# The last two units ahead of three norms in halves of the tokens, and low parts in the raw weights' place

## What is computed

```
def _rms_norm(x, g):
    return x * lax.rsqrt(jnp.mean(x * x, axis=-1, keepdims=True) + NORM_EPS) * g

def _layer(x, st, P, l):
    xn = _rms_norm(x, P['norm_mix_pre'][l])
    cols = xn @ P['w_in'][l]
    ...
    mix = merged @ P['w_out'][l]
    x = x + _rms_norm(mix, P['norm_mix_post'][l])
    xn = _rms_norm(x, P['norm_ffn_pre'][l])
    gate, up = _split(xn @ P['w_ffn_in'][l], [D_FF, D_FF])
    f = (silu(gate) * up) @ P['w_ffn_out'][l]
    x = x + _rms_norm(f, P['norm_ffn_post'][l])
```

## Time and profile before

| | us |
|---|---|
| median of 3 runs | 2446.35 (2445.53 to 2447.68) |
| the profiled execution | 2449.73 |
| its span, first to last instruction | 2447.9 |
| TensorE busy | 2335.9 |
| VectorE, ScalarE, GpSimd busy | 994.4, 863.1, 786.7 |
| granted TensorE clock, mean | 0.977 |

### The profile page before, as it was taken

One profiled execution on the slowest core, in us unless ns is written; L12 is line 12 of the kernel. 1 busy time (PEld: TensorE's weight loads), 2 busy tenths in 40 slices (PEclk: granted clock), 3 DMA queues, 4 the chain that ended last, 5 costly groups with the idle time before them and its releaser, 6 DMA issues.

```text
span 2447.9 us, 53310 instructions
## 1 busy us (share of the span) xinstructions
PE 2335.9 (95%) x23450; PEld 2224.4 (91%) x23450; DVE 994.4 (41%) x1559; ACT 863.1 (35%) x1442; POOL 786.7 (32%) x630
## 2 busy tenths in 40 slices
PE   7999989999999899999989999999999989999997
PEld 7998878988899899999989988888888989999997
DVE  4435654454434522220073376455443624332102
ACT  4345532213344522222244455222313544222222
POOL 3432322112235244444424332221212433444441
PEclk9999989999999999999989999999999999999998
DMA  5432211111124132233325221112113242332331
GB/s 164 128 88 74 57 40 32 28 49 32 42 69 145 58 90 87 87 91 87 83 93 136 61 74 53 32 28 49 32 28 83 68 129 61 90 92 87 88 88 52
DMA packets 334190, 180.80 MB, mean 74 GB/s; under 512 B 33528, under 2 KB 330648, under 8 KB 332936
## 3 DMA queue, kind: packets, MB, share of 16 engines
q1 hardware_dynamic: 333776, 177.34, 26.1%
q10 hardware_dynamic: 184, 0.05, 0.0%
HBM read 167.98 MB, written 9.38 MB: 72 GB/s over the span
## 4 chain that ended last, share of the span: by engine, by line
PE 82%; DVE 11%; ACT 4%; issue 2%; DMA 1%; POOL 0%; DVEq 0%; ACTq 0%; SPq 0%; POOLq 0%
PE psum_products L658 72%; PE psum_mixer L658 8%; DVE xn_low L2050 1%; DMA w_raw<-in_w_in 1%; DVE merged L2044 1%; DVE squares L1641 1%; DVE gate_product L2042 1%; DVE xn_low L1638 0%; ACT c_in_rate L1222 0%; ACT w_high L1222 0%; ACT c_kprime L1222 0%; DVE c_kappa_r L1753 0%; DVE c_in_rate L1754 0%; ACT L1222 0%; PE psum_mixer L1037 0%
## 5 line engine op out<-in xcount | busy, mean ns | idle before, releaser
L2273 POOL TENSOR_TENSOR w_low<-w_raw,w_high 128x512 fp32r<-128x512 f32 (+2 forms) x606 | 761.8, 1279 | 1557.7 <-ACT w_high L1222 1557.1
L658 PE MATMUL psum_products<-xn_high,w_high 128*128 128x272 f32 (+1 forms) x3424 | 738.6, 297 | 28.8 <-DVE xn_low L1623 12.3
L658 PE MATMUL psum_products<-xn_high,w_low 128*128 128x272 f32 (+1 forms) x3424 | 710.7, 289 | 0.0
L658 PE MATMUL psum_products<-xn_low,w_high 128*128 128x272 f32 (+1 forms) x3424 | 708.9, 289 | 0.0
L658 PEld LDWEIGHTS psum_products<-xn_high,w_high 128*128 128x128 f32 x3424 | 542.9, 189 | 50.6 <-issue 26.2
L658 PEld LDWEIGHTS psum_products<-xn_low,w_high 128*128 128x128 f32 x3424 | 543.0, 190 | 0.0
L658 PEld LDWEIGHTS psum_products<-xn_high,w_low 128*128 128x128 f32 x3424 | 539.7, 190 | 0.0
L1222 ACT ACTIVATE w_high<-w_raw 128x1024 fp32r<-128x1024 f32 (+2 forms) x303 | 303.2, 1003 | 174.6 <-PE psum_products L658 144.3
L658 PE MATMUL psum_products<-hidden_high,w_high 128*128 128x272 f32 x704 | 145.9, 288 | 0.0
L658 PE MATMUL psum_products<-hidden_high,w_low 128*128 128x272 f32 x704 | 145.7, 288 | 0.0
L658 PE MATMUL psum_products<-hidden_low,w_high 128*128 128x272 f32 x704 | 145.1, 288 | 0.0
(11 more groups left out here) (374 smaller groups left out, 3008.9 us busy)
## 6 DMA issues: line engine op xcount, KB each, us to landing
w_raw<-in_w_in SPq DMA_DIRECT2D x112, 512.0 KB, 4.0
w_raw<-in_w_ffn_in SPq DMA_DIRECT2D x88, 512.0 KB, 3.8
w_raw<-in_w_ffn_out SPq DMA_DIRECT2D x32, 512.0 KB, 3.9
w_raw<-in_w_out SPq DMA_DIRECT2D x16, 512.0 KB, 4.0
w_raw<-in_w_ffn_out SPq DMA_DIRECT2D x16, 384.0 KB, 3.4
x_kept<-x SPq DMA_DIRECT2D x2, 2176.0 KB, 7.5
x<-x_kept SPq DMA_DIRECT2D x2, 2176.0 KB, 9.7
w_raw<-in_w_in SPq DMA_DIRECT2D x16, 256.0 KB, 3.9
```

The costliest lines, as they stand in the source:

```text
L658: return pe.matmul(out, lhsT, rhs, start=start, stop=stop, skip_group_check=True)
L2273: low_ready.inc(pool.tensor_tensor(wl[:, n % NSPLIT, ks_], wraw[:, slot, ks_], wh[:, n % NSPLIT, ks_].bitcast(F32), ALU.subtract))
```

## The change

1. The last two units ahead of a `norm_post` (`mix` 6 and 7; of `ffn_out` block 7 its parts 1 and 2) run in halves of the tokens (`two_halves`): all of the first unit and of the second for tokens 0 to 271, then the same for tokens 272 to 543, with each half's ones-sums between. Three norms are halved; the last one, ahead of the output, is not.
2. `norm_post` on VectorE and the `norm_pre` behind it take blocks 0 to 5 for the first half, blocks 0 to 5 for the second half, then blocks 6 and 7 whole (`STEPS`, 14 steps in place of 8). Ln and Exp are taken for each half by itself; ScalarE evacuates the second half of the last unit, and takes its Ln and Exp, between the third and the fifth step.
3. `w_low` has the memory of `w_raw`: GpSimd writes the low part over the raw weights. NRAW = 5, NSPLIT = 4, splits up to unit u + 4, and a raw slot is free when its product is done. `split_both` is gone; the splits that fell there are issued by ScalarE inside `norm_pre` at block 6 ("midst").
4. `cols_a` 16 loads 32 and 96 columns where it loaded 4 and 4.

```diff
-NRAW, NSPLIT = 3, 3
+NRAW, NSPLIT = 5, 4
...
+BY_HALF = 6
+BOTH = (0, 1)
+STEPS = [(k, (0,)) for k in range(BY_HALF)] + [(k, (1,)) for k in range(BY_HALF)] + [(k, BOTH) for k in range(BY_HALF, KD)]
+def halved(l, w_):
+    return w_ in (1, 3) and (l, w_) != (DEPTH - 1, 3)
+def steps_from(l, w_):
+    return [(k, BOTH) for k in range(KD)] if (l, w_) == (0, 0) else STEPS
+def by_halves(s):
+    return (s[0] == "mix" and s[2] >= KD - 2 and halved(s[1], 1)
+            or s[0] == "ffn_out" and s[2] == KD - 1 and s[3] >= 1 and halved(s[1], 3))
...
-    wraw = fixed("w_raw", [P, NRAW, 8, P])
+    wraw_at = region(4 * NRAW * 8 * P)
+    wraw = place("w_raw", [P, NRAW, 8, P], wraw_at)
-    wl = fixed("w_low", [P, NSPLIT, 8, P], F32R)
+    wl = place("w_low", [P, NRAW, 8, P], wraw_at, F32R)
...
-        ahead, made = {}, 3
+        ahead, made = {}, 4
-                upto = sum(unit_no[t] <= u + (3 if s in split_no else 2) for t in split_units)
+                upto = sum(unit_no[t] <= u + 4 for t in split_units)
-                if plan[i + 1][0] == "norm_post":
-                    at_ = plan[i + 1]
+                if by_halves(s):
+                    at_ = ("midst", s[1] + (s[0] == "ffn_out"), 2 if s[0] == "mix" else 0)
-                ahead[at_] = list(range(made, max(made, upto)))
+                ahead.setdefault(at_, []).extend(range(made, max(made, upto)))
-        by_vec = [n for i, s in enumerate(plan) if s[0] == "norm_post" for n in ahead[s]]
...
-                return [cols(a["w_in"], 4 * A_W, A_H, 0), cols(a["w_in"], 4 * A_W + A_H, A_H, 32)]
+                return [cols(a["w_in"], 4 * A_W, 32, 0), cols(a["w_in"], 4 * A_W + A_H, 96, 32)]
...
-            def gemm(s, rh=None, rl=None, rhs=None, first=True, last=True, cut=HALF, wait_k=False, k0=0, nk=8, steps=8):
-                ks = range(done_k.get(s, 0), min(nk, done_k.get(s, 0) + steps))
+            def gemm(s, rh=None, rl=None, rhs=None, first=True, last=True, cut=HALF, wait_k=False, k0=0, nk=8, steps=8,
+                     bs=BOTH, late=False):
+                there = done_k.get((s, bs[0]), 0)
+                ks = range(there, min(nk, there + steps))
-                done_k[s] = ks[-1] + 1
+                for b in bs:
+                    done_k[s, b] = ks[-1] + 1
...
-                                  (wl[:, slot, k], rh[:, k0 + k])]
+                                  (wl[:, unit_no[s] % NRAW, k], rh[:, k0 + k])]
+                            if b not in bs:
+                                continue
-                    products.inc(last_mm)
+                    if 1 in bs:
+                        products.inc(last_mm)
+                    elif last:
+                        flow("first_half").inc(last_mm)
-            def product(s, steps=8):
+            def product(s, steps=8, bs=BOTH, late=False):
...
-                bank[0].claim(pe)
-                bank[1].claim(pe)
-                for k in range(KD):
+                for i, (k, bs) in enumerate(steps_from(l, w_)):
-                        product(s, 1)
-                    pe.wait_ge(sq_ready.sem, norm_base(l, w_) + k + 1)
-                    for b in range(2):
+                        product(s, 1, bs, late=(l, w_) != (0, 0))
+                    if i == 1 and (l, w_) != (0, 0):
+                        last_sum(*((l, 1) if w_ == 2 else (l - 1, 3)), 1)
+                    pe.wait_ge(sq_ready.sem, norm_base(l, w_) + i + 1)
+                    for b in bs:
+                        if k == 0:
+                            bank[b].claim(pe)
...
-            def post_sums(l, w_):
+            def post_sums(l, w_, bs=BOTH, wait=True):
-                flow("squares_added").wait_next(pe, "pe")
-                bank[0].claim(pe)
-                bank[1].claim(pe)
-                for b in range(2):
+                if wait:
+                    flow("squares_added").wait_next(pe, "pe")
+                for b in bs:
+                    bank[b].claim(pe)
+                for b in bs:
+            def last_sum(l, w_, b):
+                src = squares if w_ == 1 else sq2
+                if b == 0:
+                    flow(f"first_squares_{w_}").wait_next(pe, "pe", 2 if w_ == 1 else 1)
+                else:
+                    flow("last_squares").wait_next(pe, "pe")
+                bank[b].filled(mm(mp[b][:, 0:HALF], C("ones"), src[:, KD - 1, b * HALF:(b + 1) * HALF], start=False), "act")
+            def two_halves(l, w_, one, two, nk):
+                one(8, (0,))
+                two(nk - 2, (0,))
+                post_sums(l, w_, (0,))
+                two(2, (0,))
+                one(3, (1,))
+                last_sum(l, w_, 0)
+                one(8, (1,))
+                two(nk - 2, (1,))
+                post_sums(l, w_, (1,), wait=w_ == 1)
+                two(2, (1,))
+                if halved(l, w_):
+                    return
...
+            def factor_log(w_, b):
+                dst = rstd_of(w_)
+                bank[b].read(act, "act")
+                step(fn(dst[:, tokens((b,))], mp[b][:, 0:HALF], ACT.Ln, scale=1.0 / D, bias=C("scalars", 0, 1)), bank[b].empty["act"])
+            def factor_exp(w_, b):
+                dst = rstd_of(w_)
+                step(fn(dst[:, tokens((b,))], dst[:, tokens((b,))], ACT.Exp, scale=-0.5), flow("rstd"))
+            def out_half(s, b):
+                sq, y = (squares, mixed) if s[0] == "mix" else (sq2, ffn_y)
+                if b == 0:
+                    flow("first_half").wait_next(act, "act")
+                    pair = tiles[s[:3] if s[0] == "ffn_out" else s][0]
+                else:
+                    pair = product_done(s)
+                src = gp[:, 2 * pair + b, 0:HALF]
+                name = "last_squares" if b else "first_squares_1" if s[0] == "mix" else "first_squares_3"
+                (sq_ready if b and s[2] < KD - 1 else flow(name)).inc(fn(sq[:, s[2], tokens((b,))], src, ACT.Square))
+                step(fn(y[:, s[2], tokens((b,))], src, ACT.Copy), emptied["act"] if b else None)
+            def norm_post(l, w_):
+                if not halved(l, w_):
+                    factor(rstd_of(w_))
+                    return
+                factor_log(w_, 0)
+                factor_exp(w_, 0)
+                if w_ == 1:
+                    out_half(("mix", l, KD - 2), 1)
-                for k in range(KD):
+                post = (l, 1) if w_ == 2 else (l - 1, 3)
+                for i, (k, bs) in enumerate(steps_from(l, w_)):
+                    n = tokens(bs)
-                    xh_ready.inc(fn(hi[:, k, :], x[:, k, :], ACT.Copy, scale=prm[:, l, g0 + k:g0 + k + 1]))
-                    sq_ready.inc(fn(squares[:, k, :], x[:, k, :], ACT.Square))
-                    if l == 0 and w_ == 0 and k < 3:
+                        if i == 2:
+                            out_half(("mix", l, KD - 1) if w_ == 2 else ("ffn_out", l - 1, KD - 1, 2), 1)
+                    xh_ready.inc(fn(hi[:, k, n], x[:, k, n], ACT.Copy, scale=prm[:, l, g0 + k:g0 + k + 1]))
+                    sq_ready.inc(fn(squares[:, k, n], x[:, k, n], ACT.Square))
+                    if l or w_:
+                        if i == 2:
+                            factor_log(post[1], 1)
+                        if i == 3:
+                            factor_exp(post[1], 1)
+                        if k == BY_HALF and bs == BOTH:
+                            for u in ahead.get(("midst", l, w_), ()):
+                                split_high(u)
+                    elif k < 4:
...
-            def split_both(n):
-                s = split_units[n]
-                dve.wait_ge(products.sem, unit_no[split_units[n - NSPLIT]] + 1)
-                at, value = landed_at[s]
-                dve.wait_ge(landed[at].sem, value)
-                nk, slot = nk_of(s), n % NSPLIT
-                raw = wraw[:, unit_no[s] % NRAW, 0:nk]
-                step(dve.tensor_copy(wh[:, slot, 0:nk], raw))
-                step(tt(wl[:, slot, 0:nk], raw, wh[:, slot, 0:nk].bitcast(F32), SUB), vec_ready)
-                for n in ahead[("norm_post", l, w_)]:
-                    split_both(n)
+                order = STEPS if halved(l, w_) else [(k, BOTH) for k in range(KD)]
+                second = order.index((0, (1,))) if halved(l, w_) else None
-                def scaled(k):
-                    step(stt(out=tmp[:, k, :], in0=src[:, k, :], scalar=prm[:, l, g0 + k:g0 + k + 1], in1=rstd[:],
+                def scaled(i):
+                    k, bs = order[i]
+                    n = tokens(bs)
+                    if i == second:
+                        flow("rstd").wait_next(dve, "dve")
+                    step(stt(out=tmp[:, k, n], in0=src[:, k, n], scalar=prm[:, l, g0 + k:g0 + k + 1], in1=rstd_of(w_)[:, n],
-                for k in range(KD):
-                    step(tt(x[:, k, :], x[:, k, :], tmp[:, k, :], ADD), flow("x_new"))
-                    if k + 1 < KD:
-                        scaled(k + 1)
+                for i, (k, bs) in enumerate(order):
```

(57 more changed lines are left out.)

57 lines of the change are left out of this document (31 added, 26 removed).

## The result

The changed kernel takes 2454.3 us (median of 11 executions, 2452.2 to 2462.7), the kernel before 2447.7 (11, 2445.1 to 2453.3). The ratio is 1.003, with a 95% interval of 1.0018 to 1.0042: some 7 us slower. The forecast was 2453.3. The profiled execution has a span of 2452.5 us.

A forecast was written before the change was run, and what follows sets the result against it. TensorE, busy 95% of the span, bounds the kernel. Norm stages +3.4, clock +4.5, weight ring -2.0 and +1.0 make +6.9 us on the profiled 2449.73, which lies 3.4 above the median: 2453.3, own range 2449 to 2459, wider range 2437 to 2464.

The forecast's parts named there:

- The wait at the turn: TensorE's idle time between the last product and the norm's first step goes, 6.8 us a norm, and the clock stays up.
- The half step of 1.64 us: In the norm stage VectorE sets the pace, not TensorE: twelve half steps of 1.64 us, 19.7 in place of 14.6.
- ScalarE's detours: Half steps three to five: evacuating the second half, two table loads, Ln and Exp delay the roundings by 2.8 us.
- The tail: Full step 6 of the norm stage: two weight splits and the Ln table ahead of the last rounding, 2.4 us late.
- GpSimd, 0.4: GpSimd's low parts beside the norm's last steps slow VectorE by 0.4 us, bounds 0 and 0.9.
- The sums: Norm stages at full clock: mix norm 44.2 against 43.1 us, ffn norm 43.0 against 41.8; three norms +3.4.
- The clock behind the tail: TensorE idles about 2.5 us ahead of its last step; slow clock then costs 1.5 us a norm (0 to 3.0).
- The ring: The new weight slots: -2.0 for an earlier load, +1.0 for late landings, 0 for waits in the third mixers.
- (a): First layer: the weight load ScalarE stood 11.1 us for is issued a whole queue earlier, -2.0 us.
- (b): Third branch's stage: mix weights' splits find loads about 1 us short, big low parts run beside VectorE's; 0.5 a layer, +1.0.
- (c): Third mixers, 340 to 645: TensorE's waits for low parts, 4.5 us a layer, give back 0 of 9.0.
- The faster one: Norm stages: ScalarE's delays and late splits don't hold VectorE up and the clock stays; -12 in all, 2434; chance 0.20.

The follow-up runs named there:

- factor2_dve: Changed kernel with the second half's factor left out: two linear VectorE instructions replace ScalarE's inverse root, so part of the computation is missing; 2454.3 us.
- splits_last: Changed kernel with the two weight splits of a norm's full step 6 issued behind the stage's last rounding and squares; 2449.15 us.
- ring_only: Kernel before with only the new weight ring (five raw slots holding the low part, four high slots) and wider columns of cols_a 16; 2447.75 us.
- half4_last: Changed kernel with four blocks in halves, not six, and the norm's two weight splits behind the stage's last squares; 2448.9 us.
- by_half_4: Changed kernel with four blocks in halves and four whole behind each norm, in place of six and two; 2455.5 us.
- half4_last_root: half4_last with all norm factors made by square root on ScalarE and reciprocal on VectorE in place of Ln and Exp; 2442.9 us.
- ring_moved: ring_only with two weight splits a layer issued later, behind the second mixer's last chunk and the third mixer's first steps; 2448.3 us.

## Why the prediction came out, point by point
- **The wait at the turn goes.** Right in place, and the clock at the turn stays up; it is at 0.50 from 811 to 813.5, behind waits of up to 1.2 us, where VectorE sets the pace. But TensorE's idle time is the same, in nine waits.
- **The half step of 1.64 us, VectorE as the pace.** Exact: 1.64 in the chain, the half add 0.44, scale and low part 0.50. By the Trainium skill's 60 ns (Perfetto Trace Analysis, "Optimizing Scalar/DVE Operations") I had estimated 0.39 for the add, and the trace doesn't agree. I had passed over what the same passage adds, that a profiled instruction shows about twice this overhead: with 120 ns the estimate is 0.42, near the measured 0.44.
- **ScalarE's detours, 2.8 us late.** From the third add to the fifth rounding's end it is 802.62 to 809.64, 7.0 us against 6.7: 3.2 late. factor2_dve, which takes out the two tables and Ln and Exp, wins 1.2 to 1.3 us a stage at like clock, not the 1.9 that I then expected of it.
- **The tail, 2.4 late.** The last two roundings end 4.75 us apart (4.8 forecast), TensorE's gap is 2.3 (2.5). splits_last shows that the splits make 2.1 of it.
- **GpSimd, 0.4.** 0.3 in place, so the term was right for this order of issue, and its upper bound of 0.9 for one instruction was right as well. What I didn't see is that the tail kept the other instructions out of it: with the splits earlier it is 3.7 us of VectorE's time and 2.65 of the stage's. The Trainium skill (SBUF — State Buffer, "SBUF: two separate sides") has the two engines take turns on a port pair for whole instructions; 1.7 in place of 0.75 us, and back at 0.79 when GpSimd's work is cut to an eighth, agree with it.
- **The sums.** Without the clock's part the stages grew by 1.8, 1.8 and 2.0, where I had 1.1, 1.2 and 1.1: the term that was too small, by 2.2 in all. In the first norm two of its parts make up the miss: the first scale comes 11.0 us behind mix 6's first matmul (787.40 to 798.42) where I had 10.4, and the detours are 0.4 over.
- **The clock behind the tail, 1.5 each.** 1.6 behind the first norm, 1.5 behind the second (12 matmuls and the sums against 1.78 and 0.92), nothing behind the third, with the same gap: 3.1 of 4.5.
- **The ring, -2.0, +1.0 and 0.** (a) was -3.0. (b) was named wrongly: not landings in the merge stage, but whole splits ahead of a_out_high and c_tanh_w, 2.4 to 2.9 us a layer. Of (c) 2.1 us a layer came back, not nothing. I had put a change of over 3 us in the mixers' length as a sign against me: from the third mixer's first step to its last group's it is 4.2 in the changed kernel, but only 1.0 in ring_only, which has the same work there, so most of the 4.2 belongs to that execution. The parts summed to -1.0; ring_only gives 0.0, with an interval of -2.2 to +2.4, so the sum stands and its parts don't.
- **The total.** The forecast was 1.0 us low, and that it is so near is luck, since three errors cancel: the stages came to +8.8 for +7.9, the rest of the profiled execution to -4.2 for -1.0, and the profiled execution is itself the median now, where I had taken 3.4 off. The norms' costs and their places, the larger part of the forecast, are what was right.
- **The rivals.** The faster one, whose time should read 2433 for 2434 by its own sum, needed tail and detours without effect: they are there in the chain. With the tail gone (splits_last, half4_last) the kernel is where it was before, not faster.

## What to carry to other kernels
Halving a stage to cover one wait pays only while the slower engine's instructions shrink with it: here the fixed 155 ns of each VectorE instruction, the second set of table loads and the moved splits together cost 6.5 us more than the covered wait gave. With those splits moved behind the stage and four blocks in halves the stages were 4.0 us shorter than before (half4_last), and the time was the same. Work that is put off to make room lands on another chain; look what it stands ahead of, and which engine it shares a port with, before choosing its place. Where a kernel waits little, a gain of a few us must be read with the granted clock beside it: what looked like by_half_4's win in the stages was the clock's alone.

## What the runs showed of the hardware
- VectorE instructions with two inputs in SBUF took 1.67 to 1.76 us in place of 0.72 to 0.79 beside GpSimd, on 272 elements 1.26 to 1.40 in place of 0.44 to 0.50: the delay is about the same for each instruction, 0.8 to 1.0 us, whatever its length, so that work cut in halves has twice as many to suffer.
- A reciprocal on VectorE took 1.85 us for 272 elements, an add 0.44.
- The granted clock fell or stayed behind the same wait in different kernels' executions: a gap of 2.3 us ahead of the last step cost 1.6, 1.5 and 0 us at the three norms of the changed kernel's trace and 1.5, 0 and 1.4 in factor2_dve's, and a fall at 660 us cost 4.6 in one trace and did not come in the other. Executions of one kernel differ by up to 12 us (half4_last_root).
- A table load on ScalarE took 1.28 us, and each change between Ln and Exp had one: 63 loads where the kernel before has 57.
- Time and clock moved against each other: ring_only and ring_moved have 5 and 6 us less in time times clock than the kernel before, and the same time. That the clock gives back what shorter waits win is what these means suggest; no run forced the clock, so it is not shown.
